# Up-projections of keys and values as three rounded products each, with the remainders made on VectorE

## The reference

```python
q_a, c_kv, q_idx, k_idx, w_idx, q_b, k_b, v_b = jnp.split(x @ w_in, cuts, axis=-1)
o_a = dsa_attention(q_a, rms_norm(c_kv, kv_norm), q_idx, k_idx, w_idx, w_uk, w_uv)
# in dsa_attention, per query: the top 64 keys by a ReLU index, then
q_lat = einsum('bshd,hdr->bshr', q, w_uk);  logits = einsum('bqhr,bqkr->bqhk', q_lat, c_sel) / 8 - alibi
o     = einsum('bqhr,hrd->bqhd', softmax(logits) @ c_sel, w_uv)
```

## Time and profile before

| | us |
|---|---|
| median of 3 runs (lowest, highest) | 600.83 (600.82, 600.89) |
| the profiled execution | 600.68 |
| its span in the profile | 598.9 |
| TensorE busy | 591.4 |
| VectorE busy | 423.0 |
| ScalarE busy | 343.0 |

### The profile page before, as it was taken

How to read it: one execution, slowest core, us unless ns; L and a number is a source line. 1 busy time by engine, 2 the same in 40 slices (tenths; PEclk the granted TensorE clock), 3 DMA queues, 4 the chain that set the end, 5 groups by cost and what they waited for, 6 DMA issues and landing times.

```text
span 598.9 us, 9656 instructions
## 1 busy us (share of the span) xinstructions
PE 591.4 (99%) x3387; PEld 508.5 (85%) x3387; DVE 423.0 (71%) x694; ACT 343.0 (57%) x644; POOL 27.3 (5%) x49
## 2 busy tenths in 40 slices
PE   9999999999999999999999999999999999999995
PEld 7988887888888888888888898888888888888885
DVE  4699868878566656556888878768675665666547
ACT  5777977466445554545557667635664455455530
POOL 1111111100000000000010000002000000000000
PEclk9999999999999999999999999999999999999999
DMA  8757427377655555664448543662766556555401
GB/s 314 257 179 266 141 71 252 100 253 246 237 180 187 195 177 182 202 200 151 144 137 281 178 134 121 210 198 85 266 218 193 186 184 207 194 178 190 140 1 70
DMA packets 30112, 109.43 MB, mean 183 GB/s; under 512 B 3376, under 2 KB 3376, under 8 KB 29952
## 3 DMA queue, kind: packets, MB, share of 16 engines
q1 hardware_dynamic: 28512, 102.77, 51.9%
q0 software_dynamic: 1568, 6.23, 3.2%
HBM read 107.94 MB, written 1.05 MB: 182 GB/s over the span
## 4 chain that ended last, share of the span: by engine, by line
PE 99%; DVE 0%; DVEq 0%; issue 0%; ACT 0%; POOL 0%; ACTq 0%; POOLq 0%
PE bank L1209 27%; PE bank L1120 25%; PE bank L1123 13%; PE bank L1638 5%; PE bank L1473 3%; PE bank L1642 3%; PE bank L1113 2%; PE bank L1187 2%; PE bank L1632 2%; PE bank L1162 2%; PE bank L1163 2%; PE bank L1169 2%; PE bank L1304 1%; PE bank L1315 1%; PE bank L1295 1%; PE bank L1477 1%
## 5 line engine op out<-in xcount | busy, mean ns | idle before, releaser
L737 DVE TENSOR_TENSOR wlo<-raw,whi 128x1024 fp32r<-128x1024 f32 x190 | 226.9, 1224 | 50.0 <-ACT whi L367 49.5
L367 ACT CAST whi<-raw 128x1024 fp32r<-128x1024 f32 x190 | 192.5, 1049 | 12.0 <-DMA raw<-stream_in 11.0
L1120 PE MATMUL bank<-hTs,whi 128*128 128x512 f32 x640 | 159.9, 392 | 0.0
L1120 PEld LDWEIGHTS bank<-hTs,whi 128*128 128x128 f32 x640 | 116.2, 189 | 21.6
L1123 PEld LDWEIGHTS bank<-hTs,wlo 128*128 128x128 f32 x640 | 87.3, 190 | 6.2
L1209 PE MATMUL bank<-whi,oThi 128*128 128x512 f32 x234 | 92.2, 394 | 0.0
L1209 PE MATMUL bank<-whi,oTlo 128*128 128x512 f32 x234 | 91.3, 390 | 0.0
L1209 PE MATMUL bank<-wlo,oThi 128*128 128x512 f32 x234 | 91.1, 389 | 0.0
L1123 PE MATMUL bank<-hTs,wlo 128*128 128x256 f32 x640 | 89.2, 282 | 0.0
L630 ACT COPY kT<-bank 128x256 f32<-128x256 f32 x40 | 14.9, 372 | 69.6 <-PE bank L1123 69.6
L1014 DVE TENSOR_TENSOR kT<-bank,kT 128x256 f32<-128x256 f32 x40 | 17.0, 425 | 51.9 <-ACT kT L630 51.8
(11 more groups left out here) (192 smaller groups left out, 722.5 us busy)
## 6 DMA issues: line engine op xcount, KB each, us to landing
raw<-stream_in SPq DMA_DIRECT2D x190, 512.0 KB, 4.6
qT<-ln_rows_in POOLq DMA_DIRECT2D x8, 512.0 KB, 4.9
kT<-stream_in SPq DMA_DIRECT2D x2, 512.0 KB, 5.4
v<-xT_in SPq DMA_DIRECT2D x2, 512.0 KB, 5.4
h<-x_in POOLq DMA_DIRECT2D x1, 1024.0 KB, 7.2
out<-h SPq DMA_DIRECT2D x4, 256.0 KB, 2.1
dist<-consts_in POOLq DMA_DIRECT2D x1, 384.0 KB, 3.4
ukv<-w_uk_in POOLq DMA_DIRECT2D x1, 256.0 KB, 6.5
```

The source lines that it names most:

```text
L367: nc.scalar.copy(whi[:, c % RING, j * HW:(j + 1) * HW], raw[:, c % RAW, j * HW:(j + 1) * HW]).then_inc(whi_ready, 1)
L737: nc.vector.tensor_tensor(wlo[:, c % RING, cols], raw[:, c % RAW, cols], whi[:, c % RING, cols].bitcast(F32), ALU.subtract).then_inc(wlo_r ...
L1120: mm(dst[:], whi[:, slot, off + k * P:off + (k + 1) * P], hTs[:, k].rearrange("p j s -> p (j s)"), start=(k == 0), stop=False)
```

## The change

The operands of both up-projections become a rounded high part and a low remainder each, and each product becomes three. The high parts are written by ScalarE: the two copies that were there now write rounded values, and a cast of the value weights is added ahead of them. The remainders are three new subtractions on VectorE, put between the two halves of the split of chunk 5. All six parts lie in `oThi` and `oTlo`. TensorE waits for both parts of the keys' operands ahead of the keys and for both parts of the value weights ahead of the values.

```diff
+        turned_uk, turned_c = bank[6][:], bank[7][:, S:2 * S]
+        ukT, cT, wv = ([o[:, a:b].rearrange("p k s -> p (k s)") for o in (oThi, oTlo)]
+                       for a, b in ((0, 2), (2, 3), (3, 5)))
...
 # ScalarE
             split_hi(5)
+            act.wait_ge(par_loaded, 48)
+            nc.scalar.copy(wv[0], ukv[:, 1].rearrange("p a b -> p (a b)")).then_inc(wv_ready, 1)
             act.wait_ge(ukT_done, 1)
-            nc.scalar.copy(ukT, bank[6][:]).then_inc(ukT_ready, 1)
+            nc.scalar.copy(ukT[0], turned_uk).then_inc(ukT_ready, 1)
             act.wait_ge(ctr_done, 1)
-            nc.scalar.copy(cT, bank[7][:, S:2 * S]).then_inc(cT_ready, 1)
+            nc.scalar.copy(cT[0], turned_c).then_inc(cT_ready, 1)
...
 # VectorE
             topk_round(0)
-            split_lo(5)
+            split_lo_half(5, 0)
+            dve.wait_ge(ukT_ready, 1)
+            nc.vector.tensor_tensor(ukT[1], turned_uk, ukT[0].bitcast(F32), ALU.subtract).then_inc(ukT_ready, 1)
+            dve.wait_ge(cT_ready, 1)
+            nc.vector.tensor_tensor(cT[1], turned_c, cT[0].bitcast(F32), ALU.subtract).then_inc(cT_ready, 1)
+            dve.wait_ge(wv_ready, 1)
+            nc.vector.tensor_tensor(wv[1], ukv[:, 1].rearrange("p a b -> p (a b)"), wv[0].bitcast(F32), ALU.subtract
+                                    ).then_inc(wv_ready, 1)
+            split_lo_half(5, 1)
             topk_round(1)
...
 # TensorE
-            pe.wait_ge(ukT_ready, 1)
-            pe.wait_ge(cT_ready, 1)
+            pe.wait_ge(ukT_ready, 2)
+            pe.wait_ge(cT_ready, 2)
             for j in range(4):
-                last = mm(bank[6 + j // 2][:, (j % 2) * S:(j % 2 + 1) * S], ukT[:, j * P:(j + 1) * P], cT,
-                          start=True, stop=True)
+                for i, (w, a) in enumerate(((0, 0), (0, 1), (1, 0))):
+                    last = mm(bank[6 + j // 2][:, (j % 2) * S:(j % 2 + 1) * S], ukT[w][:, j * P:(j + 1) * P], cT[a],
+                              start=(i == 0), stop=(i == 2))
             last.then_inc(kA_done, 1)
+            pe.wait_ge(wv_ready, 2)
             for t in range(2):
-                last = mm(bank[2 + t][:], cT[:, t * P:(t + 1) * P], ukv[:, 1].rearrange("p a b -> p (a b)"),
-                          start=True, stop=True)
+                for i, (a, w) in enumerate(((0, 0), (0, 1), (1, 0))):
+                    last = mm(bank[2 + t][:], cT[a][:, t * P:(t + 1) * P], wv[w], start=(i == 0), stop=(i == 2))
             last.then_inc(vA_done, 1)
```

More of the change, by code:

```diff
@@ L102, in build @@
         qiT = early[:, 0:2 * S].rearrange("p (k s) -> p k s", s=S)
-        kiT, cT = early[:, 2 * S:3 * S], early[:, 3 * S:4 * S]
-        ukT = early[:, 4 * S:6 * S]
+        kiT = early[:, 2 * S:3 * S]
         cn = early[:, 6 * S:7 * S].rearrange("p (t c) -> p t c", t=2)
@@ L169, in build @@
         moved = sem("moved")
+        wv_ready = sem("wv_ready")
         stored, rows_done = sem("stored"), sem("rows_done")
```

## The result

The changed kernel takes 601.50 us (median of 20 runs, 600.88 to 602.41), the kernel before 600.74 (20 runs, 600.24 to 601.67). The ratio is 1.0014 with a 95% interval of 1.0008 to 1.002: slower by some 0.8 us, where 0.0 was forecast. The profiled execution after has a span of 600.1 us (598.9 before). Just ahead of the edit, TensorE and VectorE lie 0.17 to 0.19 us later in it than in the one before: the key-weight transposes start at 29.74 instead of 29.55, VectorE's first selection round at 29.24 instead of 29.06.

What follows compares the result with a forecast made beforehand. The prediction took TensorE (busy 99%) as the bound, with VectorE saturated from 37.06 to 61.50 us. Its terms, -0.63 + 0.30 + about 0.33 = 0.0 us, gave 600.8 us, own range 600.5 to 601.2.

Steps and rivals of the forecast that it cites:

- TensorE's gain: Key and value products on TensorE: 3.45 us of fp32 products replaced by 2.82 us of rounded ones, 0.63 us gained.
- the estimate of 0.86: Same products on TensorE, by the skill page's pass rule alone: three passes take three quarters, 2.59 us, gain 0.86 us.
- ScalarE's cast: Added cast of the value weights on ScalarE, 0.6 us: fits into 0.71 us of idle time and costs nothing.
- VectorE's remainders: Three added subtractions on VectorE between the halves of chunk 5: 0.60 + 0.33 + 0.60 = 1.53 us.
- the delay behind the idle time: VectorE at 37.06 us: its 0.95 us wait absorbs part of the remainders, leaving it 0.50 us late.
- First place: TensorE at 46 us, second half of chunk 5, waits for ScalarE's previous evacuation, moved 0.50 later: 0.30 us lost.
- Second place: TensorE at 60.83 us, second half of chunk 7, waits for VectorE's late add: about 0.33 us, the remaining lead, lost.
- VectorE's short wait at 58.77: VectorE's wait for a ScalarE cast ending at 58.73 us: takes back 0.20 us of VectorE's 0.50 us delay.
- rival two: VectorE's lag wins at its add ahead of chunk 7's second half: slower, 601.4 to 601.7 us; chance 0.18.

Runs made afterwards that it cites:

- highs_only: Changed kernel without the three remainders on VectorE, all 18 products on the high parts (low products left out of the result): 600.59 us.
- dead_remainders: Kernel before, with its fp32 products, plus the three remainder subtractions on VectorE with their results unused: 601.35 us.
- v_copy: Changed kernel with one of VectorE's two value copies given to ScalarE: 600.82 us, ratio to the kernel before 0.9998.
- pool_wv: Changed kernel, value weights' cast earlier on ScalarE, their remainder on GpSimd: 602.22 us; second run also with chunk 4's evacuation ahead of the mask-waiting casts: 602.67 us.
- late_cast: Changed kernel with one useless 128x1024 copy on ScalarE ahead of the cast of chunk 7's first half: 602.91 us.

## Why the prediction was wrong

By its steps. **TensorE's gain** 0.63: measured 0.63, so the estimate of 0.86 beside it was too high. **ScalarE's cast**: free, as said. **VectorE's remainders** 1.53: measured 1.53, and the delay behind the idle time 0.50: measured 0.69 with the start's 0.17, so 0.52. TensorE waited for no remainder.

**First place**, forecast loss 0.30: measured 1.26 (0.44 early to 0.82 late). This is the step that failed: "All of that moves 0.50 later". It took the duration of GpSimd's mask, 1.47 us of the earlier trace rows, as the mask's own and moved it along. It is 0.41 of work and a wait for VectorE's first split. The casts of the splits are made by ScalarE, which came early with TensorE while VectorE came late, so the head start of the second split grew from 0.31 to 1.27 us. The mask, which had gone ahead of the second split, now waited for both and grew by 1.0. Either half is enough: with early casts alone (highs_only) or late remainders alone (dead_remainders) the mask took as long. The evacuation was forecast for 45.63 and ended at 46.79: 0.17 of start, 0.99 of mask.

**Second place**, forecast loss 0.33: measured 0, since TensorE came there 0.8 late instead of 0.33 early. The runs show that it would have cost more than forecast as well. The prediction counted VectorE's short wait at 58.77 (0.20) as slack that pays for lag; it was the pause that let the second pair's masks in. In the 18 profiled executions of this study those masks took 0.87 or 0.88 us in each of the 11 in which the split began 0.09 us or more after the sums, and 1.79 or 1.80 in each of the 7 in which it followed at once. The split at 58.77 that takes 1.46, which rival two prices, is longer because it waits for the second of these masks (58.75 to 59.15).

So the sum is -0.63 + 1.26 + 0.0 = 0.63 on the stretch, where 62.71 - 62.05 = 0.66 was measured. The two profiled executions differ by more, 1.2 us: 0.18 lie ahead of the stretch and 0.35 behind it, and no run shows that these come from the change; the medians differ by 0.76. **Rival two** had the sign, and 601.50 lies inside its 601.4 to 601.7, but that is luck: it had neither the place nor the mechanism, as it put VectorE's lag at the add. v_copy speaks against it: no lag on VectorE, the lead lost all the same.

The Trainium skill, SBUF — State Buffer, section Who interferes with whom, says that a VectorE instruction with two inputs in SBUF contends with a GpSimd instruction that reads SBUF, that the lock is exclusive, and that the later one is blocked outright. The traces agree: splits (two inputs in SBUF) shut the mask out for 1 or 2 times 1.2 us; sums and copies with an input in PSUM did not (0.41 each). From the earlier trace rows alone, the 1.47 us could have been read as a wait for the first split. That the mask would be passed over by the second split as well, which made the 1.0 us, is in no row of the kernel before.

What stays open is why the head start decides. GpSimd went ahead of the second split in the three cases with 0.31 and 0.39 us (before, and the two pool_wv runs, where it was a subtraction and not a mask), and was passed over in all ten with 0.49 us or more. late_cast was to bring the head start down to 0.25 us in the changed kernel; its execution had 0.79.

## What to carry to other kernels

When a short instruction shows a long duration in the profile (a mask at 0.41 us in one place and 1.47 in another), find out what runs beside it before you move it: part of that duration can be a wait that depends on another engine's pauses. A short idle moment of a saturated engine, or an input that comes only just in time, may be what lets another engine through; making its inputs earlier can then make the kernel slower, and an explicit wait at that point, or work from PSUM in between, can make it faster. Where a chain passes two such places, freeing one shows the other: test them together.

## What the runs showed of the hardware

- A mask of 128x256 on GpSimd took 0.41 us alone, 1.33 to 1.47 with one of VectorE's 128x1024 subtractions in its way and 2.47 with two; one of 128x16 took 0.21 alone and 2.26 with two. The profile books the wait as busy time, of GpSimd and of VectorE alike (a split took 1.42 or 2.32 us instead of 1.21).
- A subtraction of 128x512 on GpSimd shows 2.26 us, of which some 1.1 are a wait for VectorE's split and 1.16 its own work; it held up VectorE's next split by 1.1 us.
- A subtraction of VectorE whose input had been ready for 0.49 us or more when the one before it ended went ahead of a waiting GpSimd instruction in ten of ten cases; with 0.31 and 0.39 us GpSimd went first in three of three.
- In single executions ScalarE waited up to 3.1 us for the load of one early half (late_cast), with no edit near it, where the profiled executions before and after show no wait; VectorE then ran up to 1.4 us later against TensorE.
